# Gate and z products of a two-block transformer kernel as three fp32r products each, with the low parts made by GpSimd

## The reference, cut to what matters

```python
def hybrid_mixer(h, w_in, gate_b, ...):
    proj = h @ w_in
    y_a = short_conv_mixer(proj[..., SC_OFF:SB_OFF], sc_conv_w)
    ...
    y_b = stick_breaking_attention(q.reshape(hs), k.reshape(hs), v.reshape(hs))
    y_c = rwkv7_mixer(proj[..., RW_OFF:SG_OFF], ...)
    y_d = spatial_gating(proj[..., SG_OFF:GATE_OFF], sg_ln_g, sg_ln_b, sg_w, sg_b)
    gates = jax.nn.sigmoid((proj[..., GATE_OFF:] + gate_b).astype(jnp.float32)).astype(h.dtype)
    gates = gates.reshape(bsz, t, N_BRANCH, D_MODEL)
    merged = (gates[:, :, 0] * (y_a @ sc_out) + gates[:, :, 1] * (y_b @ sb_out)
              + gates[:, :, 2] * (y_c @ rw_out) + gates[:, :, 3] * (y_d @ sg_out))
    return merged @ w_o
```

## Time and profile before

| | |
|---|---|
| median of 3 runs | 1658.9 us (1658.85 to 1659.67) |
| the profiled execution | 1661.19 us, its span 1659.4 us |
| PE, PEld busy | 97%, 88% of the span |
| DVE, ACT, POOL busy | 70%, 48%, 21% |
| low part on POOL (median of 79) | 2.42 us |
| low part on DVE (median of 44) | 1.22 us |
| high part on ACT (median of 76) | 1.05 us |

### The profile page before, as it was taken

One profiled execution on the slowest core, in us unless ns is written; L12 is line 12 of the kernel. 1 busy time (PEld: TensorE's weight loads), 2 busy tenths in 40 slices (PEclk: granted clock), 3 DMA queues, 4 the chain that ended last, 5 costly groups with the idle time before them and its releaser, 6 DMA issues. The chain is left out here.

```text
span 1659.4 us, 33473 instructions
## 1 busy us (share of the span) xinstructions
PE 1606.3 (97%) x11586; PEld 1463.2 (88%) x11586; DVE 1158.1 (70%) x2293; ACT 795.3 (48%) x1323; POOL 355.2 (21%) x229
## 2 busy tenths in 40 slices
PE   7999998999998999999999999999999999999997
PEld 6987887899998987789999999999999888888886
DVE  5463315777787787726599996777774677777776
ACT  5252113555554473243555553555555555555554
POOL 1030000034442003358568990000000000000000
PEclk9999999999999999999999999999999999999999
DMA  7513334255664421154548775555557777677763
GB/s 286 158 62 104 103 105 150 91 191 188 182 187 167 166 77 64 41 188 160 172 168 235 212 221 172 177 180 178 175 176 222 249 239 239 227 239 237 240 228 125
DMA packets 92809, 289.52 MB, mean 174 GB/s; under 512 B 10304, under 2 KB 27072, under 8 KB 92352
## 3 DMA queue, kind: packets, MB, share of 16 engines
q1 hardware_dynamic: 92304, 287.61, 54.4%
q10 hardware_dynamic: 432, 0.90, 0.2%
HBM read 270.65 MB, written 17.83 MB: 174 GB/s over the span
## 5 line engine op out<-in xcount | busy, mean ns | idle before, releaser
L262 PE MATMUL psum<-arena_parts 128*128 128x256 f32 (+2 forms) x1664 | 478.9, 288 | 25.5 <-DVE ring_parts L257 12.0
L264 PE MATMUL psum<-arena_parts,ring_parts 128*128 128x256 f32 (+1 forms) x1600 | 451.2, 282 | 0.0
L2703 DVE TENSOR_TENSOR ring_parts<-ring,arena_parts 128x512 fp32r<-128x512 f32 x418 | 282.7, 690 | 113.7 <-ACT arena_parts L2497 95.3
L262 PEld LDWEIGHTS psum<-arena_parts 128*128 128x128 f32 x1664 | 316.0, 190 | 28.4 <-DVE ring_parts L257 11.1
L264 PEld LDWEIGHTS psum<-arena_parts,ring_parts 128*128 128x128 f32 x1600 | 305.4, 191 | 0.0
L263 PE MATMUL psum<-h_parts,arena_parts 128*128 128x256 f32 x1024 | 286.9, 280 | 0.0
L257 POOL TENSOR_TENSOR ring_parts<-ring,arena_parts 128x1024 fp32r<-128x1024 f32 x79 | 209.9, 2680 | 65.8 <-ACT arena_parts L253 47.1
L233 PE MATMUL psum<-h,ring 128*128 128x256 f32 x896 | 205.5, 387 | 0.0
L2466 PE MATMUL psum<-arena_parts,x_parts 128*128 128x512 f32 x512 | 201.1, 393 | 1.2 <-DVE x_parts L2730 1.2
L2467 PE MATMUL psum<-ring_parts,x_parts 128*128 128x512 f32 x512 | 201.5, 394 | 0.0
L2468 PE MATMUL psum<-arena_parts,x_parts 128*128 128x512 f32 x512 | 201.2, 393 | 0.0
(11 more groups left out here) (539 smaller groups left out, 2868.6 us busy)
## 6 DMA issues: line engine op xcount, KB each, us to landing
ring<-stream SPq DMA_DIRECT2D x473, 512.0 KB, 3.6
kept<-arena SPq DMA_DIRECT2D x128, 128.0 KB, 2.3
arena<-kept SPq DMA_DIRECT2D x32, 512.0 KB, 4.3
arena<-first SPq DMA_DIRECT2D x1, 2144.0 KB, 16.7
arena<-second SPq DMA_DIRECT2D x1, 1632.0 KB, 6.7
x<-x_t SPq DMA_DIRECT2D x1, 1024.0 KB, 5.8
out<-arena SPq DMA_DIRECT2D x4, 256.0 KB, 2.1
arena<-last ACTq DMA_DIRECT2D x1, 512.0 KB, 3.4
```

The source lines that it names most:

```text
L262: nc.tensor.matmul(dst, stationary[0], moving[0], start=first, stop=False)
L264: return nc.tensor.matmul(dst, stationary[1], moving[0], start=False, stop=last_one)
L2703: v.tensor_tensor(low[:, s, w], ring[:, s, w], expert_high[:, m % 2, w].bitcast(F32), ALU.subtract)\
```

## The change

A new SBUF array `rounded` holds four blocks of high parts. Gate and z blocks go through `three` (24 fp32r matmuls) with the parts of the weights and of h.

- ACT adds one high part a block (128 x 1024): `gate_high(g + 3)` right behind its read of gate g, three of them at the end of the stage before; `z_high(g + 2)` ahead of its read of z block g, once the products of block g are done.
- POOL makes all 32 gate lows: three in the stage before, 3 and 4 between the halves of the short convolution, the rest behind it. It makes z's lows 0 to 9 ahead of the pair loop, and 10 to 17 one behind each pair. DVE makes the last six.
- h is split once for the gates (ACT 2, DVE 2 operations) and once for z (ACT 2, POOL 2).
- Some gate blocks change their place in PE's queue: one goes between the products for spatial gating and the wait for `sb_weights`, others into the end of the stage; the last read goes to the next stage.
- The counts of semaphores follow; the last stage takes an older semaphore in place of its own, and the kernel is built with a smaller scratch for DMA descriptors (`dynamic_dma_scratch_size=1024`).

```diff
+        rounded = sb("rounded", [P, 4, D], F32R)
...
         def part_low(eng, ns, high, s, number):
-            eng.wait_ge(S("high"), number)
+            eng.wait_ge(S("high"), number + split["apart"])
...
+        gate_h = Area(arena_parts[(P + EARLY) * T], 2048).take(KT, T)
+        gate_h_low = h_parts[:, :, 0:T]
+        made = {}
+        GATES, gate_base = 32, split["blocks"] + 24
         n_norm, squares_base = normed["n"], normed["squares"]
...
+        def gate_high(act, g):
+            part_high(act, rounded, g % 4, 4 + g // 4)
+
+        def gate_low(eng, ns, g):
+            eng.wait_ge(S("high"), gate_base + g + 1)
+            ns.tensor_tensor(low[:, g % 4, :], ring[:, g % 4, :], rounded[:, g % 4, :].bitcast(F32), ALU.subtract)\
+                .then_inc(S("gate_low"), 1)
 
...
+                for g in range(3):
+                    gate_low(pool, nc.gpsimd, g)
...
+                            made["h"] = vec.n
+                for half in range(2):
+                    k = slice(4 * half, 4 * half + 4)
+                    dve.wait_ge(S("h_rounded"), KT + half + 1)
+                    v.tensor_tensor(gate_h_low[:, k, :], h[:, k, 0:T], gate_h[:, k, :].bitcast(F32), ALU.subtract)\
+                        .then_inc(S("h_parts"), 1)
...
+                act.wait_ge(S("vector_step"), made["h"])
+                for half in range(2):
+                    k = slice(4 * half, 4 * half + 4)
+                    nc.scalar.activation(gate_h[:, k, :], h[:, k, 0:T], ACT.Copy).then_inc(S("h_rounded"), 1)
+                for g in range(3):
+                    gate_high(act, g)
...
+        def gate_parts(q, w, b, i):
+            g = gate_n["pe"]
+            s = g % 4
+            nc.tensor.wait_ge(S("gate_low"), g + 1)
+            if g == 0:
+                nc.tensor.wait_ge(S("h_parts"), split["h"])
+            for k in range(KT):
+                c = slice(k * P, (k + 1) * P)
+                ins = three(b[:, 0:T], (rounded[:, s, c], low[:, s, c]), (gate_h[:, k, :], gate_h_low[:, k, :]),
+                            k == 0, k == KT - 1)
+            return ins
+
         def gate_products(pe, n):
             for _ in range(n):
                 s = gate_n["pe"] % 4
-                project(pe, [s], [s % 2], 1, channels(T))
+                project(pe, [s], [s % 2], 1, gate_parts)
                 gate_n["pe"] += 1
 
...
+                if g + 3 < GATES:
+                    gate_high(act, g + 3)
...
+                    if c == 0:
+                        for n in (3, 4):
+                            gate_low(pool, g, n)
                 poo.eng.sem_inc(S("short_conv"), 1)
+                for n in range(5, GATES):
+                    gate_low(pool, g, n)
...
-                gate_reads(act, 2)
-                for b in range(2):
-                    act.wait_ge(drained[b], ev_at.banks[b] + 1)
+                gate_reads(act, 1)
...
                 ins.then_inc(S("sg_mixed"), 1)
+                gate_products(pe, 1)
                 pe.wait_ge(S("sb_weights"), 1)
...
-                gate_products(pe, 3)
+                gate_products(pe, 2)
...
+                gate_products(pe, 1)
                 pe.wait_ge(S("level_grown"), LEVELS)
...
-                gate_products(pe, 2)
+                gate_products(pe, 1)
...
-                gate_products(pe, 3)
+                gate_products(pe, 1)
...
+                    if ch == 1:
+                        gate_products(pe, 1)
                 pe.wait_ge(S("rw_y"), 1)
                 mm(bank[5][:, :], f("same"), y0.rearrange("p c t -> p (c t)"), start=True, stop=True)\
                     .then_inc(S("gn_mean"), 1)
+                gate_products(pe, 1)
                 pe.wait_ge(S("gn_squares"), 1)
                 mm(bank[6][:, :], f("same"), yd2.rearrange("p c t -> p (c t)"), start=True, stop=True)\
                     .then_inc(S("gn_var"), 1)
                 gate_products(pe, 2)
 
...
+                gate_reads(act, 1)
+                for b in range(2):
+                    act.wait_ge(drained[b], ev_at.banks[b] + 1)
...
+        z_h = rounded[:, 2:4, :].rearrange("p a n -> p (a n)").rearrange("p (k t) -> p k t", t=T)
+        z_h_low = h_parts[:, :, M:TT]
+        Z_BLOCKS, BY_POOL, gates_low = 24, 18, GATES
+        z_filled = [pe_at.rounds[s] + 4 for s in range(4)]
+        z_base, z_h_base = split["blocks"] + 12, split["h"] + 4
+
+        def z_high(act, g):
+            if g < Z_BLOCKS:
+                act.wait_ge(full[g % 4], (z_filled[g % 4] + g // 4) * 16)
+                nc.scalar.activation(rounded[:, g % 2, :], ring[:, g % 4, :], ACT.Copy).then_inc(S("high"), 1)
+
+        def z_low(eng, ns, g):
+            eng.wait_ge(S("high"), split["apart"] + z_base + g + 1)
+            ns.tensor_tensor(low[:, g % 4, :], ring[:, g % 4, :], rounded[:, g % 2, :].bitcast(F32), ALU.subtract)\
+                .then_inc(S("gate_low") if g < BY_POOL else S("low"), 1)
+
+        def z_parts(q, w, b, i):
+            g = proj_n["pe"]
+            if g < BY_POOL:
+                nc.tensor.wait_ge(S("gate_low"), gates_low + g + 1)
+            else:
+                nc.tensor.wait_ge(S("low"), z_base + g - BY_POOL + 1)
+            if g == 0:
+                nc.tensor.wait_ge(S("h_parts"), z_h_base + 2)
+            for k in range(KT):
+                c = slice(k * P, (k + 1) * P)
+                ins = three(b[:, 0:T], (rounded[:, g % 2, c], low[:, g % 4, c]), (z_h[:, k, :], z_h_low[:, k, :]),
+                            k == 0, k == KT - 1)
+            return ins
+
         def z_products(pe, n):
             for _ in range(n):
                 g = proj_n["pe"]
-                project(pe, [g % 4], [z_bank(g)], 1, channels(T, M))
+                project(pe, [g % 4], [z_bank(g)], 1, z_parts)
                 proj_n["pe"] += 1
 
         def z_reads(act, n, func=ACT.Copy):
             for _ in range(n):
                 g = proj_n["act"]
+                if g + 2 < Z_BLOCKS:
+                    act.wait_ge(used[g % 4], ev_at.rounds[g % 4] + 1)
+                    z_high(act, g + 2)
                 evacuate(act, [g % 4], [z_bank(g)], 1, lambda q, b, i: nc.scalar.activation(zg[:, g, :], b[:, 0:T], func))
                 proj_n["act"] += 1
 
...
+                for half in range(2):
+                    k = slice(4 * half, 4 * half + 4)
+                    pool.wait_ge(S("h_rounded"), z_h_base + half + 1)
+                    g.tensor_tensor(z_h_low[:, k, :], h[:, k, M:TT], z_h[:, k, :].bitcast(F32), ALU.subtract)\
+                        .then_inc(S("h_parts"), 1)
+                for n in range(10):
+                    z_low(pool, g, n)
...
+                    z_low(pool, g, 10 + p)
...
-                        if n == 9:
+                        if n % 2:
...
+                for n in range(BY_POOL, Z_BLOCKS):
+                    z_low(dve, v, n)
...
+                    if n > 9:
+                        half = n - 10
+                        k = slice(4 * half, 4 * half + 4)
+                        act.wait_ge(h_scaled, ONCE + half + 1)
+                        a.activation(z_h[:, k, :], h[:, k, M:TT], ACT.Copy).then_inc(S("h_rounded"), 1)
                 silu(0)
+                z_high(act, 0)
+                z_high(act, 1)
...
-                pe.wait_ge(h_scaled, ONCE + 1)
...
+    nc = bacc.Bacc("TRN2", target_bir_lowering=False, num_devices=1, dynamic_dma_scratch_size=1024)
```

More of the change, by code:

```diff
@@ L244, in tokens @@
             return mm
-        split = {"blocks": 0, "h": 0}
+        split = {"blocks": 0, "h": 0, "apart": 0}
         low = ring_parts
@@ L486, in build @@
             split["blocks"] += 24
-            split["h"] += KT
+            split["h"] += KT + 2
         a2 = Area(arena, scratch_at)
@@ L969, in _ @@
                 gate_products(pe, 2)
+        split["apart"] += GATES
         a5 = Area(arena, scratch_at)
@@ L1027, in ff_low @@
             s, filled, number = ff_block(n, i)
-            dve.wait_ge(S("high"), number)
+            dve.wait_ge(S("high"), number + split["apart"])
             nc.vector.tensor_tensor(low[:, s, :], ring[:, s, :], high[:, s, :].bitcast(F32), ALU.subtract)\
@@ L2027, in build @@
             ev_at.advance((4, 5, 6), 1, None)
-            split["blocks"] += 12
-            split["h"] += 4
+            split["blocks"] += 12 + Z_BLOCKS - BY_POOL
+            split["apart"] += BY_POOL
+            split["h"] += 6
             normed["squares"] += 2
@@ L2742, in build @@
         last_g = a_end.take(D)
+        last_in = S("meta_in")
         with nc.Block() as block:
@@ L2745, in _ @@
             def _(act):
-                act.dma_start(last_g, last).then_inc(S("last_in"), 16)
+                act.dma_start(last_g, last).then_inc(last_in, 16)
                 for b in range(4):
@@ L2764, in _ @@
                 dve.wait_ge(S("last_root"), 1)
-                dve.wait_ge(S("last_in"), 16)
+                dve.wait_ge(last_in, 32)
                 for b in range(4):
@@ L2909 @@
```

(2 more changed lines are left out.)

## The result

The changed kernel takes 1680.2 us (median of 4 runs, 1678.2 to 1683.9) against 1658.9: a ratio of 1.0125, 95% interval 1.0112 to 1.0138, so 21 us slower. I had forecast 1667, in a range of 1641 to 1677. The direction was right, the size too small by 13 us, and the time lies above the range. The profiled execution took 1678.4 us (span 1676.6).

What follows compares the result with a forecast made beforehand. PE, busy 97%, was taken as the bound except where DVE chains end later. Profiled 1661.2 - 8.6 (mixers) + 16.5 (second block) = 1669.1, or 1666.8 with the median 2.3 us lower; forecast 1667 us, range 1641 to 1677.

Steps and rivals of the forecast that it cites:

- What bounds, and the saving of a block: PE bounds except where a DVE chain ends later; a split block takes 2.81 us, saving 0.645 us.
- 13.5 + 6.0 + 1.7: Mixers' gains: 13.5 us from 21 cheaper gate blocks, 6.0 from filling the tail's gaps, 1.7 from its clock.
- Holds in the mixers: Six POOL lows hold DVE's L638 to L655 for 2.1 us each, +12.6 us on sb_weights and the attention output.
- Holds ahead of the loop: Second block before the head loop: eleven of twelve new POOL instructions hold DVE 1.5 us each, +16.5 us.
- The failed step: Second block's head loop: eight lows meet mostly PSUM operations, 0.3 us a head, +1.2 us; far bound 16.8.
- the last blocks' -1.2: z blocks 16 to 23: -5.2 us from cheaper products, +4.0 us because blocks 17 and 18 wait for their parts.
- The clock, left out of the sum: The head loop's sum had no clock loss; one rival had 3.4 us each at two places outside the loop.
- the new waits and the loop: Rival: PE idles for sb_weights and ahead of the loop, clock loses 7 us, loop lows 6: 1680 us; chance 0.10.
- The rival without holds: Whole kernel: DVE is in front in most meetings, so lows wait and not DVE: 1634.6 us, faster; chance 0.13.

Runs made afterwards that it cites:

- short memsets: Changed kernel with each gate low part, and each z low part by POOL or DVE, replaced by one 128x1024 memset that reads nothing: 1631.8 us, ratio 0.9815.
- long memsets: Kernel with memsets for low parts, but POOL takes three memsets per low part, about the subtraction's length; DVE's last six are real: 1643.7 us, ratio 0.9898.

## Why the prediction was right in kind and too low

- *What bounds, and the saving of a block*: right. Where PE was the bound the gates gave what was counted: from L850's place (9.6 us late: 140.23 to 149.80) to the feed-forward norm (11.6 early) the mixers won 21 us, against my 13.5 + 6.0 + 1.7 = 21.2.
- *Holds in the mixers*: right in mechanism, six counted, five came, of 2.0 us: 10 us for 12.6. This is most of the 3 us by which the gates did better.
- *Holds ahead of the loop*: +16.5 forecast, 16.2 found (12.7 early to 3.5 late). Nine holds of 1.9 us where I had eleven of 1.5; the sum was the same, partly by luck. My 1.5 was 2.1 less every fourth operation, which "has one input or is tiny"; four of the nine holds were on just such operations, L1650 (128x16) among them, so that reason was wrong. z block 5 waited 4.6 us and not 2.9, beside DVE's chain, and the clock of 0.87 from 572 to 626 us, which I had not counted, took 7 us, most of it hidden behind that chain: L2052 still waits 3.3 us for DVE at its end.
- **The failed step**: "In the loop eight lows meet mostly operations with a PSUM operand (L1700): I take 0.3 us a head, +1.2 us", together with the last blocks' -1.2. Measured: 3.5 to 16.4 us late, +12.9, where the two terms sum to 0: the loop is 11.4 us longer (90.6 to 102.0) and the last blocks 1.5. I had judged the loop by one row, L1700 with its PSUM operand. But of the eight lows, two met `finish_head` (L1688) and three L1661, which have their inputs in SBUF. In the lines of DVE of the changed kernel, 626 to 750 us, L1782 (L1688 of before) takes 8.7 us for 4.0 and L1755 (L1661) 7.5 for 3.5, so 8.7 us of holds where I had 1.2; the lines of before, 622 to 735 us, follow:

```profile
L1782 DVE SCALAR_TENSOR_TENSOR arena<-arena,par 128x256 f32<-128x256 f32 x8 | 8.7, 1132 | 0.7 <-ACT arena L1938 0.6
...
L1755 DVE TENSOR_TENSOR arena<-arena 128x272 f32<-128x272 f32 x8 | 7.5, 942 | 0.0
```

```profile
L1688 DVE SCALAR_TENSOR_TENSOR arena<-arena,par 128x256 f32<-128x256 f32 x8 | 4.0, 540 | 0.7 <-ACT arena L1835 0.6
...
L1661 DVE TENSOR_TENSOR arena<-arena 128x272 f32<-128x272 f32 x8 | 3.5, 432 | 0.0
```

- *The clock, left out of the sum*: this is the second half of the failed step, a term that the sum has at nothing in the loop. There PE idles 9.6 us (102.0 - 92.4), 8.7 more than before, and loses 10.2 us at a clock of 0.90; ten blocks give back 6.5. That is +12.4, against a window that is 11.4 us longer than before's. 8.0 us of the idle time are waits for DVE and 1.6 are a block's wait for its low part. The clock alone is as large as all the idle time. Clock and loop holds stood in my rival "the new waits and the loop", with 1680 us and a chance of 0.10. Its two ingredients are what happened, but not where it put them: it had 3.4 us of clock behind each of the waits for sb_weights and ahead of the loop, and the loss came inside the loop (behind the mixers' wait it was 1.9 us). That its 1680 is the measured time is luck in part.
- *The rest of the 13.4 us by which 1666.8 missed*: mixers -3.0, ahead of the loop -0.3, loop and last blocks +12.9, from there to L1910 -1.1 and the stages behind +0.8, for which I have no cause, and +4.1 because the profiled execution was 2.3 us above the median before and is 1.8 below it after.
- *The rival without holds* (1634.6) was what the chip gives once POOL reads nothing: 1631.8 with short and 1643.7 with long memsets. Its condition, that the low waits and not DVE, did not hold; that its number is met within 3 us by the short memsets is partly luck, since these also hand their parts over sooner.

The traces divide the loop's loss into idle time and clock, but how far held operations cause the fall of the clock was not tried apart: no run had the holds without it. That it falls at all where PE's waits are this short stays unexplained; before, the loop had waits of 0.30 us only and a clock of 1.00.

## What to carry to other kernels

An idle GpSimd isn't free: here an elementwise operation on it that read SBUF stopped VectorE operations with two SBUF inputs, and scalar operations and casts with one, for up to its own length. So look at what VectorE does at that moment before giving work away, and read each place, not one row for a whole loop. Put such work where VectorE is idle or on PSUM operands; here holding the low parts back past one chain and leaving the second block alone turned 21 us lost into 18 gained. And where TensorE gets a new wait of 1 to 3 us, leave room for what its clock takes behind it: in the loops of these kernels that was as much as all the new idle time (10.2 to 8.7 us) or three times as much (8.2 to 2.7), and behind two single waits four to five times the wait.

## What the runs showed that I had not expected

- A wait of PE of 2.03 us was followed by 17 us at a granted clock of 0.52 (8 us lost), one of 1.19 us by 13 us at 0.56; 1.2 GHz is the lower of the two levels, 0.5 of full speed. But 6.2 us of waiting in the mixers were followed by 0.69 over 6 us only (144 to 150 us), so the cost does not go with the length of the wait.
- The loop loses 10 us to 19 us of reads by POOL even when nothing depends on POOL's work.
- GpSimd writes 128x1024 in 0.95 us, against 2.4 us for the subtraction, and neither one memset nor a string of them slowed VectorE's operations with two SBUF inputs; a copy and a scalar operation were held for 0.7 us by one.
